# Gate spreads as one 256-column product per token, and the end of stage E

## The chip, the cores and the metric

The kernel runs on one core of a Trainium2 chip. The metric is the device time of one execution in microseconds. The five engines that matter are TensorE (PE in the profile, PEld for its weight loads), VectorE (DVE), ScalarE (ACT), GpSimd (POOL) and the transfer queues, of which most are filled by SyncE (SP).

## What is computed

One layer of a decoder over 520 tokens (512 of a prompt, 8 of a decoding batch): attention and a state-space layer, then a mixture of 16384 single-neuron experts, 128 x 128, chosen by product keys. The change touches the mixture alone:

```python
def peer(h, w_q, sub_keys, u_tab, v_tab):
    ...
        s1, i1 = lax.top_k(s[:, :, 0], PEER_TOPK)
        s2, i2 = lax.top_k(s[:, :, 1], PEER_TOPK)
        ...
        top_s, top_p = lax.top_k(cand_s, PEER_TOPK)
        idx = jnp.take_along_axis(cand_i, top_p, axis=-1)
        gate = jax.nn.softmax(top_s, axis=-1)
        u = u_tab[idx]
        act = jax.nn.gelu(jnp.einsum('thkd,td->thk', u, hb).astype(jnp.float32))
        v = v_tab[idx].astype(jnp.float32)
        return jnp.einsum('thk,thkd->td', gate * act, v).astype(h.dtype)
```

Each token has 8 heads with 16 chosen experts each, 128 (first key, second key, gate) triples.

## The kernel before, in words

The program has five stages one behind the other, with a barrier and a clearing of semaphores between any two. A, M and D are the projections, attention and state space, and the output projection. Stage E makes the query products and the first half of the mixture, stage F the second half and the last norm.

All dense products split an operand into a part in the rounded 32-bit format (float32r) and a rest in the same format, and add three products: high x high, low x high, high x low. A block of weights (1 MB, a "unit") is loaded by SP into `raw`, ScalarE writes its rounded part `wh` in two halves (`split_hi`, L122), GpSimd subtracts it in four instructions of 128 x 512 into the rest `wl` (`split_lo`, L129), TensorE multiplies. Two units are in flight: ScalarE starts on unit u + 2 when TensorE has finished unit u.

The mixture treats tokens in two ways. 360 of the 520 tokens are dense: in stage E TensorE forms their product with each of the 16384 expert rows of u (128 units, `dense`, L1560 to L1570, 48 products of 360 columns each), ScalarE applies the gelu (L1483) and stores the result to memory (L1485). For the other 160 (128 "A" tokens and 32 "x" tokens) the chosen rows are gathered one per token and step by an indirect transfer that GpSimd issues (L1423 and L1430, 128 steps each, spread over the units by `gathers_by`), into rings of four buffers (`GW`, `GX`). VectorE forms their dots (`dot`, L1729, 2048 elements against PSUM; `dot_x`, L1736, 512 elements, both inputs in SBUF). The gather of step k waits for the dot of step k - 4.

The dense tokens need their gates as a full 128 x 128 matrix per token. `spread` builds it on TensorE: for one token the stationary operand holds, for each of its 128 chosen triples, a row that is one at the second key, the moving operand a row that is the gate at the first key. `one_hots` (L1738 to L1749) makes both on VectorE by comparing a line of 0..127, kept in PSUM, with the triple's numbers. There are 90 batches of four tokens, one behind each of 90 units of stage E, in three groups of thirty (`batch_of`, units 16 to 109 with two free ones between groups). The products are 32-bit ones of 128 columns, and TensorE carries each out as two records. ScalarE copies the four results from PSUM to `gs` (L1512) with a stride, and stores `gs` after every six batches (L1516). `keyrow` has two sets of rows, so `one_hots` of batch b waits for the spread of batch b - 2. VectorE's order of a unit in the code is: dots, dots of x, compares, and in eight units a piece of the choice for the next group of tokens (`offer_choice`, L1702 to L1705).

Stage E ends with the split of the second block of stage F, the sum of x's partial dots on TensorE (L1621), two gelus on ScalarE (L1518, L1520) and two multiplications by the gates on VectorE (L1794, L1796). Stage F begins with loads on SP, the weighing of the first eight stored rows (VectorE L2004, ScalarE L1899, VectorE L1977, one behind another), then runs 128 units like E's against the rows of v, with three `raw` buffers.

Of the kernel before, what the change touches and what calls it, by code (L numbers as in the profile page):

```python
# [8 lines left out]
F32 = mybir.dt.float32  # L9
# [8 lines left out]
P = 128  # L18
# [50 lines left out]
def common(nc, ctx, ins, outs):  # L69
# [18 lines left out]
    m.gains = at("gains", [P, 3, KT]); m.eps = at("eps", [P, 1]); m.pages = at("pages", [1, P], I32); m.lam = at("lam", [P, 8])  # L88
# [1266 lines left out]
def stage_e(nc, m, ins, outs):  # L1355
# [10 lines left out]
    act0, g0, actx, gX, pf, tpa, p0 = row("act0", 0), row("g0", 1), row("actx", 2), row("g_x", 3), row("pf", 4), row("tpa", 5, U32), [row("p00", 6), row("p01", -1)]  # L1366
# [3 lines left out]
    m.idxx = at("idxx", [P, HK], I32); m.wx = at("wx", [P, HK]); m.xsel = at("xsel", [P, P + 1])  # L1370
# [16 lines left out]
    S = {n: sem("e_" + n) for n in "keys_in iota_in root_ready h_ready h_hi h_lo tok_turned tok_kept query_ready scored scores_kept head_taken chain idx_ready h_placed iota_placed best_shifted exps_ready choice_ready choice_turned keys_ready spread_done side_kept dotted dots_gelu gates_stored x_turned x_kept x_dotted x_summed xsel_in".split()}  # L1387
# [4 lines left out]
    batch_of = {E0 + SPAN * (b // per) + b % per: b for b in range(NB * BB)}  # L1392
    choice_of = {E0 - 1 + SPAN * j: j for j in range(DT)}
    piece_of = {SPAN * j - 12 + 4 * part: (j, part) for j in range(1, DT) for part in range(4)}
    with nc.Block() as block:
# [15 lines left out]
        def _(pool):  # L1411
# [22 lines left out]
        def _(act):  # L1434
# [42 lines left out]
            side = 0  # L1477
            for e in range(N_EXP):
                u, s = U_EXP_U + e, e % 2
                split_hi(m, act, u + 2, s, (u + 2) // 2, (m.mm_done, u + 3))  # L1480
# [5 lines left out]
                if e == 0:  # L1486
# [3 lines left out]
                    act.wait_ge(S["iota_in"], 16)  # L1490
                    act.activation(m.acc[:, 1, 1, 0:P], iota[:, :], ACT.Copy).then_inc(S["iota_placed"], 1)
# [6 lines left out]
                if e in choice_of:  # L1498
# [3 lines left out]
                    side += 1  # L1502
                if e in batch_of:
                    b = batch_of[e]
                    blk, n = b // BB, b % BB
                    act.wait_ge(S["spread_done"], b + 1)
                    if n == 0:
                        if blk >= 2:
                            act.wait_ge(S["gates_stored"], 16 * (blk - 1))
                        if blk == 0:  # L1510
                            act.wait_ge(S["h_placed"], 4)
# [12 lines left out]
        def _(pe):  # L1524
# [47 lines left out]
            def turn_choice(j, ready, side):  # L1572
                pe.wait_ge(S["choice_ready"], ready)
                if side is not None:
                    pe.wait_ge(S["side_kept"], side)
# [582 lines left out]
```

## Time and profile before

| | |
|---|---|
| Median of the runs shown | 3469.01 us (three: 3463.54, 3469.01, 3469.45) |
| The profiled execution, own time | 3468.28 us |
| Its span | 3466.5 us |
| TensorE busy | 3310.6 us, 96% |
| VectorE busy | 2403.1 us, 69% |
| GpSimd busy | 2286.2 us, 66% |
| ScalarE busy | 1107.3 us, 32% |
| Transfers, mean | 280 GB/s |

Stage E lies between about 1100 and 2420 us of the span, its units with spreads between 1449 and 2270 us, stage F behind 2425 us. "Busy" of TensorE is a modelled duration of overlapping products, so distances between starts are what counts. A bracket at the end of a timeline row gives the idle time before the instruction and what ended it; an x4 row is four instructions merged, with their time in all.

### The profile page before, as it was taken

The numbers are of one execution on the slowest core, as the hardware profiler recorded it, in microseconds if no ns is written. First come the engines' busy times: TensorE is split into PE (matmuls) and PEld (weight loads), VectorE is DVE, ScalarE is ACT, GpSimd is POOL, SyncE is SP. The second block draws the span as 40 slices with busy tenths as digits, with TensorE's granted clock in tenths as the row PEclk, the third lists the DMA queues.
The fourth block names the chain that finished last, engine by engine and source line by source line (L and its number), as shares of the span: only waits on it lengthen the run. The fifth ranks groups of instructions, "written<-read, shape, count | busy, mean of one in ns | idle before, by whom it ended". The sixth has DMA issues, their size and how long they took to land. (4 is left out here: it accounts for less than half of the span.)

```text
span 3466.5 us, 58063 instructions
## 1 busy us (share of the span) xinstructions
PE 3310.6 (96%) x22639; PEld 3131.8 (90%) x22639; DVE 2403.1 (69%) x4061; ACT 1107.3 (32%) x1501; POOL 2286.2 (66%) x1861
## 2 busy tenths in 40 slices
PE   7999987888998999999999999998999999999997
PEld 7988854556998999999999999998999999999997
DVE  7842323324313899998598666646799999999984
ACT  4211123234223224344444444432332232332332
POOL 2533308002443347888898888887799999999983
PEclk9999989999998999999999999999999999999998
DMA  4598977574332223788988898987998998989972
GB/s 157 191 373 312 348 293 250 212 239 164 145 118 88 85 85 135 280 327 330 345 332 341 331 346 325 347 341 279 377 381 347 382 368 359 382 355 372 375 283 98
DMA packets 239612, 970.33 MB, mean 280 GB/s; under 512 B 44913, under 2 KB 92658, under 8 KB 160626
## 3 DMA queue, kind: packets, MB, share of 16 engines
q1 hardware_dynamic: 110546, 553.25, 42.5%
q0 software_dynamic: 57344, 335.58, 24.1%
q10 hardware_dynamic: 71520, 78.87, 6.7%
q8 instruction: 119, 1.95, 0.2%
q14 instruction: 83, 0.68, 0.1%
HBM read 891.32 MB, written 73.92 MB: 278 GB/s over the span
## 5 line engine op out<-in xcount | busy, mean ns | idle before, releaser
L129 POOL TENSOR_TENSOR wl<-raw,wh 128x512 fp32r<-128x512 f32 x776 | 1049.9, 1386 | 641.7 <-ACT wh L122 640.0
L122 ACT ACTIVATE wh<-raw 128x1024 fp32r<-128x1024 f32 x396 | 397.5, 1051 | 1223.7 <-PE acc L149 581.2
L1567 PE MATMUL acc<-hh,wh 128*128 128x360 f32 x2048 | 677.5, 331 | 6.6 <-POOL wl L129 6.6
L1946 PE MATMUL acc<-vh,wh 128*128 128x360 f32 x2048 | 668.9, 327 | 12.9 <-DVE vl L1977 12.8
L1569 PE MATMUL acc<-hh,wl 128*128 128x360 f32 x2048 | 671.0, 328 | 0.0
L1948 PE MATMUL acc<-vh,wl 128*128 128x360 f32 x2048 | 670.8, 328 | 0.0
L1568 PE MATMUL acc<-hl,wh 128*128 128x360 f32 x2048 | 670.8, 328 | 0.0
L1947 PE MATMUL acc<-vl,wh 128*128 128x360 f32 x2048 | 669.2, 327 | 0.0
L1876 POOL TENSOR_TENSOR wl<-raw,wh 128x512 fp32r<-128x512 f32 x442 | 564.2, 1310 | 50.2 <-ACT wh L1914 48.2
L147 PE MATMUL acc<-hh,wh 128*128 128x256 f32 (+1 forms) x1920 | 548.5, 286 | 6.4 <-DVE tt L427 3.8
L148 PE MATMUL acc<-hl,wh 128*128 128x256 f32 (+1 forms) x1920 | 545.5, 284 | 0.0
L149 PE MATMUL acc<-hh,wl 128*128 128x256 f32 (+1 forms) x1920 | 544.1, 283 | 0.0
L1914 ACT ACTIVATE wh<-raw 128x1024 fp32r<-128x1024 f32 x252 | 253.2, 1052 | 604.7 <-PE acc L1948 546.4
L1729 DVE SCALAR_TENSOR_TENSOR ug<-ug,aux 128x2048 f32<-128x2048 f32 x128 | 291.8, 2283 | 175.2 <-DMA ug<-expert_u,idx 169.2
L1946 PEld LDWEIGHTS acc<-vh,wh 128*128 128x128 f32 x2048 | 385.5, 188 | 13.9 <-issue 12.9
L1567 PEld LDWEIGHTS acc<-hh,wh 128*128 128x128 f32 x2048 | 384.3, 188 | 9.2 <-issue 9.2
L147 PEld LDWEIGHTS acc<-hh,wh 128*128 128x128 f32 x1920 | 365.2, 190 | 22.8 <-issue 22.7
L1947 PEld LDWEIGHTS acc<-vl,wh 128*128 128x128 f32 x2048 | 385.2, 188 | 0.0
L1568 PEld LDWEIGHTS acc<-hl,wh 128*128 128x128 f32 x2048 | 385.1, 188 | 0.0
L1948 PEld LDWEIGHTS acc<-vh,wl 128*128 128x128 f32 x2048 | 385.0, 188 | 0.0
L1569 PEld LDWEIGHTS acc<-hh,wl 128*128 128x128 f32 x2048 | 384.9, 188 | 0.0
L148 PEld LDWEIGHTS acc<-hl,wh 128*128 128x128 f32 x1920 | 364.9, 190 | 0.1
(364 smaller groups left out, 5103.2 us busy)
## 6 DMA issues: line engine op xcount, KB each, us to landing
raw<-units SPq DMA_DIRECT2D x324, 1024.0 KB
kr<-cache_k SPq DMA_DIRECT2D x128, 512.0 KB, 6.6
vr<-cache_v SPq DMA_DIRECT2D x128, 512.0 KB, 5.6
expert_acts<-ast ACTq DMA_DIRECT2D x128, 180.0 KB
expert_gates<-gs ACTq DMA_DIRECT2D x15, 1536.0 KB
g<-expert_gates SPq DMA_DIRECT2D x16, 1440.0 KB, 10.7
a<-expert_acts SPq DMA_DIRECT2D x30, 720.0 KB, 13.9
output_steps<-qo ACTq DMA_DIRECT2D x16, 288.0 KB, 7.1
```

The source lines that it names most:

```text
L122: act.activation(m.wh[s][:, k:k + KT // 2, :], m.raw[s][:, k:k + KT // 2, :], ACT.Copy).then_inc(m.hi_done, 1)
L129: x = pool.tensor_tensor(m.wl[s][:, part, :], m.raw[s][:, part, :], m.wh[s][:, part, :].bitcast(F32), ALU.subtract)
L147: pe.matmul(o, m.wh[s][:, k, :], rhs_hi[:, k, c0:c0 + n], start=(k == k_range[0]), stop=False)
L148: pe.matmul(o, m.wh[s][:, k, :], rhs_lo[:, k, c0:c0 + n], start=False, stop=False)
L149: mm = pe.matmul(o, m.wl[s][:, k, :], rhs_hi[:, k, c0:c0 + n], start=False, stop=(k == k_range[-1]))
L1567: pe.matmul(o, m.wh[s][:, k, :], m.hh[:, k, N0:T], start=(k == 0), stop=False)
L1568: pe.matmul(o, m.wh[s][:, k, :], m.hl[:, k, N0:T], start=False, stop=False)
L1569: mm = pe.matmul(o, m.wl[s][:, k, :], m.hh[:, k, N0:T], start=False, stop=(k == KT - 1))
L1876: x = pool.tensor_tensor(wl[v % RW][:, part, :], raw[v % RW][:, part, :], wh[v % RW][:, part, :].bitcast(F32), ALU.subtract)
L1946: pe.matmul(tile_acc[r % AW], wh[b][:, VT * e + d, :], vh[g % 2][:, e, :], start=(e == 0), stop=False)
L1947: pe.matmul(tile_acc[r % AW], wh[b][:, VT * e + d, :], vl[g % 2][:, e, :], start=False, stop=False)
L1948: mm = pe.matmul(tile_acc[r % AW], wl[b][:, VT * e + d, :], vh[g % 2][:, e, :], start=False, stop=(e == GRP - 1))
```

## The change

The spread becomes one product per token in the rounded format with 256 moving columns: the first 128 are the key row times the gate's low part, the other 128 the key row times the gate (written rounded). The two halves of the result stand side by side in PSUM, in two banks for the four tokens of a batch. VectorE adds them while it copies them to `gs` (`keep_gates`, two reductions of 512 elements), a step that ScalarE did before. VectorE makes the key rows of four tokens with two compares of 512 elements, whose line now lies in SBUF, and ScalarE scales them by the gate's low part and by the gate (eight operations of 128 columns), waiting for the compares in the unit before. There is one set of key rows. VectorE's order of a unit becomes: keep the last batch's gates, compares, dots, dots of x, choice pieces. The store of `gs` moves one unit later.

At the seam, the split of the second block of stage F moves from E's end into F (`rest(1)` on GpSimd, its rounding on ScalarE behind the eight first roundings of the weighed rows and three loads). The sum of x's dots, the two gelus and the two multiplications move into F too: TensorE's product to its very start, the gelus behind ScalarE's rounding of unit 2, the multiplications behind VectorE's first rests. The dots are summed directly into `w0` and `wx`; the gates of the gathered tokens lie where the page table and qs were.

```diff
-    keyrow = at("keyrow", [P, KT, T], F32, off=hx + KT * T * 4)
+    keyrow = at("keyrow", [P, KT, T], F32R, off=hx + KT * T * 4)
+    glo, ghr = row("glo", 0), row("ghr", 1, F32R)
...
+    store_of = {E0 + SPAN * (blk // RUN) + BB * (blk % RUN) + BB: blk for blk in range(NB)}
-                split_lo(m, pool, u + 2, u % 2)
+                if e < N_EXP - 1:
+                    split_lo(m, pool, u + 2, u % 2)
-                split_hi(m, act, u + 2, s, (u + 2) // 2, (m.mm_done, u + 3))
+                act.wait_ge(m.mm_done, u + 3)
+                if e < N_EXP - 1:
+                    split_hi(m, act, u + 2, s, (u + 2) // 2, (m.mm_done, u + 3))
-                    act.wait_ge(S["iota_in"], 16)
-                    act.activation(m.acc[:, 1, 1, 0:P], iota[:, :], ACT.Copy).then_inc(S["iota_placed"], 1)
...
-                if e in batch_of:
-                    b = batch_of[e]
-                    blk, n = b // BB, b % BB
-                    act.wait_ge(S["spread_done"], b + 1)
...
-                    act.activation(gs[blk % 2][:, :, 4 * n:4 * n + 4].rearrange("p e t -> p t e"), m.acc[:, 0, 1, :].rearrange("p (t e) -> p t e", t=4), ACT.Copy).then_inc(S["side_kept"], 1)
-                    if n == BB - 1:
-                        act.wait_ge(S["side_kept"], side)
-                        act.dma_start(m.gD[:, :, blk, :], gs[blk % 2][:, :, :].rearrange("p (g e) n -> p g (e n)", g=NG)).then_inc(S["gates_stored"], 16)
-            act.wait_ge(S["dotted"], HK)
-            act.activation(act0[:, :], act0[:, :], ACT.Gelu_apprx_tanh).then_inc(S["dots_gelu"], 1)
-            act.wait_ge(S["x_summed"], 1)
-            act.activation(actx[:, :], m.acc[:, 0, 1, 0:HK], ACT.Gelu_apprx_tanh).then_inc(S["dots_gelu"], 1)
+                if e in store_of:
+                    blk = store_of[e]
+                    act.wait_ge(S["gates_kept"], 2 * BB * (blk + 1) + 1)
+                    act.dma_start(m.gD[:, :, blk, :], gs[blk % 2][:, :, :].rearrange("p (g e) n -> p g (e n)", g=NG)).then_inc(S["gates_stored"], 16)
+                if e + 1 in batch_of:
+                    b = batch_of[e + 1]
+                    if b % per == 0:
+                        act.wait_ge(S["gates_split"], b // per + 1)
+                    act.wait_ge(S["keys_made"], b + 1)
+                    for t in range(4):
+                        act.activation(keyrow[:, 8 + t, 0:P], keyrow[:, t, 0:P].bitcast(F32), ACT.Copy, scale=glo[:, 4 * b % DW + t:4 * b % DW + t + 1])
+                    for t in range(4):
+                        x = act.activation(keyrow[:, 12 + t, 0:P], keyrow[:, t, 0:P].bitcast(F32), ACT.Copy, scale=gt[:, 0, 4 * b + t:4 * b + t + 1])
+                    x.then_inc(S["keys_ready"], 1)
...
-            def spread(n, b, side):
+            def spread(b, j):
                 pe.wait_ge(S["keys_ready"], b + 1)
-                pe.wait_ge(S["side_kept"], side)
-                for t in range(4):
-                    r = 4 * (n % 2) + t
-                    mm = pe.matmul(m.acc[:, 0, 1, P * t:P * t + P], keyrow[:, r, 0:P], keyrow[:, 8 + r, 0:P], start=True, stop=True)
+                pe.wait_ge(S["side_kept"], j + 1)
+                for h in range(2):
+                    if h == 0:
+                        pe.wait_ge(S["gates_kept"], b * 2 + 1)
+                    for t in range(2 * h, 2 * h + 2):
+                        mm = pe.matmul(m.acc[:, h, 1, 2 * P * (t % 2):2 * P * (t % 2) + 2 * P].rearrange("p (x n) -> p x n", x=2), keyrow[:, 4 + t, 0:P], keyrow[:, 8 + t:13 + t:4, 0:P], start=True, stop=True)
                 mm.then_inc(S["spread_done"], 1)
...
-            pe.wait_ge(S["side_kept"], (per + 1) * DT)
-            pe.wait_ge(S["x_dotted"], HK)
-            pe.matmul(m.acc[:, 0, 1, 0:HK], m.xsel[:, 0:P], actx[:, :], start=True, stop=True).then_inc(S["x_summed"], 1)
+            pe.wait_ge(S["gates_kept"], 2 * per * DT + 1)
...
+                                         accum_out=m.w0[:, k:k + 1]).then_inc(S["dotted"], 1)
...
+                dve.scalar_tensor_tensor(ugx[k % GX][:, :], ugx[k % GX][:, :], 1.0, hq[:, :], ALU.mult, ALU.mult, accum_out=m.wx[:, k:k + 1]).then_inc(S["x_dotted"], 1)
+
+            def split_gates(j):
+                dve.wait_ge(S["side_kept"], j + 1)
+                ch(dve.tensor_copy(ghr[:, 0:DW], gt[:, 0, DW * j:DW * j + DW]))
+                dve.tensor_tensor(glo[:, 0:DW], gt[:, 0, DW * j:DW * j + DW], ghr[:, 0:DW].bitcast(F32), ALU.subtract).then_inc(S["gates_split"], 1)
+
+            def keep_gates(b):
+                blk, n = b // BB, b % BB
+                dve.wait_ge(S["spread_done"], b + 1)
+                if n == 0 and blk >= 2:
+                    dve.wait_ge(S["gates_stored"], 16 * (blk - 1))
+                for h in range(2):
+                    parts = m.acc[:, h, 1, :].rearrange("p (t x e) -> p t e x", t=2, x=2)
+                    dve.tensor_reduce(gs[blk % 2][:, :, 4 * n + 2 * h:4 * n + 2 * h + 2].rearrange("p e t -> p t e"), parts, AX.X, ALU.add).then_inc(S["gates_kept"], 1)
-                n = b % BB
-                if b == 0:
-                    dve.wait_ge(S["iota_placed"], 1)
-                if b >= 2:
-                    dve.wait_ge(S["spread_done"], b - 1)
-                line = m.acc[:, 1, 1, 0:P]
-                for t in range(4):
-                    c, r = 4 * b + t, 4 * (n % 2) + t
-                    dve.tensor_scalar(keyrow[:, r, 0:P], line, gt[:, 2, c:c + 1], None, ALU.is_equal)
-                    x = dve.tensor_scalar(keyrow[:, 8 + r, 0:P], line, gt[:, 1, c:c + 1], gt[:, 0, c:c + 1], ALU.is_equal, ALU.mult)
-                x.then_inc(S["keys_ready"], 1)
+                line = iota[:, :].unsqueeze(1).broadcast_to([P, 4, P])
+                for x in range(2):
+                    i = dve.tensor_tensor(keyrow[:, 4 * x:4 * x + 4, 0:P], line, gt[:, 1 + x, 4 * b:4 * b + 4].unsqueeze(2).broadcast_to([P, 4, P]), ALU.is_equal)
+                i.then_inc(S["keys_made"], 1)
...
             for e in range(N_EXP):
+                if e - 1 in batch_of:
+                    keep_gates(batch_of[e - 1])
+                if e in batch_of:
+                    b = batch_of[e]
+                    if b % per == 0:
+                        split_gates(b // per)
+                    one_hots(b)
                 while k < dots_by(e):
                     dot(k)
                     k += 1
                 while kx < dots_x_by(e):
                     dot_x(kx)
                     kx += 1
-                if e in batch_of:
-                    b = batch_of[e]
-                    if b % per == 0:
-                        dve.wait_ge(S["side_kept"], (per + 1) * (b // per) + 1)
-                    one_hots(b)
                 if e in piece_of:
                     offer_choice(*piece_of[e])
...
-            dve.wait_ge(S["dots_gelu"], 1)
-            ch(dve.tensor_tensor(m.w0[:, :], act0[:, :], g0[:, :], ALU.mult))
-            dve.wait_ge(S["dots_gelu"], 2)
-            ch(dve.tensor_tensor(m.wx[:, :], actx[:, :], gX[:, :], ALU.mult))
+            dve.wait_ge(S["dotted"], HK)
+            dve.wait_ge(S["x_dotted"], HK)
...
+            def rest(v):
+                for k in range(0, KT * 3 // 4 if rest_shared(v) else KT, KT // 4):
+                    if k % (KT // 2) == 0:
+                        pool.wait_ge(m.hi_done, (U_EXP_V + v) * 2 + (1 + 2 * k // KT))
+                    part = slice(k, k + KT // 4)
+                    x = pool.tensor_tensor(wl[v % RW][:, part, :], raw[v % RW][:, part, :], wh[v % RW][:, part, :].bitcast(F32), ALU.subtract)
+                x.then_inc(m.lo_done, 1)
+
+            rest(1)
+                    rest(j + 2)
...
+            act.wait_ge(raw_in[1], raw_count(1))
+            for k in range(0, KT, KT // 2):
+                act.activation(wh[1][:, k:k + KT // 2, :], raw[1][:, k:k + KT // 2, :], ACT.Copy).then_inc(m.hi_done, 1)
...
+            def rounded(v):
+
+            rounded(2)
+            act.activation(m.w0[:, :], m.w0[:, :], ACT.Gelu_apprx_tanh).then_inc(S["w_gelu"], 1)
+            act.wait_ge(S["x_summed"], 1)
+            act.activation(m.wx[:, :], m.acc[:, 1, 0, 0:HK], ACT.Gelu_apprx_tanh).then_inc(S["w_gelu"], 1)
+            for v in range(2, N_EXP):
+                if v > 2:
+                    rounded(v)
...
+            pe.matmul(m.acc[:, 1, 0, 0:HK], m.xsel[:, 0:P], m.wx[:, :], start=True, stop=True).then_inc(S["x_summed"], 1)
...
+            dve.wait_ge(S["w_gelu"], 2)
+            dve.tensor_tensor(m.w0[:, :], m.w0[:, :], m.g0[:, :], ALU.mult).then_inc(S["w_ready"], 1)
+            dve.tensor_tensor(m.wx[:, :], m.wx[:, :], m.gX[:, :], ALU.mult).then_inc(S["w_ready"], 1)
+            dve.wait_ge(S["w_ready"], 2)
```

## Rows read from the trace of the kernel before

**Rows 1.** The page: the span.

```profile
span 3466.5 us, 58063 instructions
```

**Rows 2.** Busy us by engine (PE, PEld, DVE, ACT, POOL), granted clock, transfers.

```profile
1449.30:1697.67 248.37, 247.61 (x1568) 247.31 (x1569) 218.99 (x388) 104.58 (x110) 214.34 (x176) 1.00 0.88 333
```

**Rows 3.** TensorE's waits, whole span: us in total, times, longest.

```profile
PE acc L1946 <- DVE vl L1977: 12.8, 1, 12.8
...
PE acc L1567 <- POOL wl L129: 6.6, 9, 1.8
```

**Rows 4.** Timeline of TensorE: two spreads (start, us, line, operation, tiles).

```profile
1600.54 1.05 PE L1585 MATMUL acc<-keyrow 128*128 128x128 f32 x8
...
1609.37 0.38 PE L1585 MATMUL acc<-keyrow 128*128 128x128 f32 x2
```

**Rows 5.** Timeline of ScalarE: gelus of the last units of E.

```profile
2407.72 0.45 ACT L1483 ACTIVATE ast<-acc 128x360 f32<-128x360 f32 x1
...
2415.66 0.45 ACT L1483 ACTIVATE ast<-acc 128x360 f32<-128x360 f32 x1
```

**Rows 6.** Timeline of TensorE: products of 256 columns, first and 36th.

```profile
1179.78 0.28 PE L148 MATMUL acc<-hl,wh 128*128 128x256 f32 x1
...
1183.93 0.28 PE L147 MATMUL acc<-hh,wh 128*128 128x256 f32 x1
```

**Rows 7.** Timeline of GpSimd around the same two spreads.

```profile
1601.32 0.95 POOL L1430 DMA_INDIRECT ugx<-expert_u,idxx  x1 [0.31 <-issue]
1602.28 5.04 POOL L129 TENSOR_TENSOR wl<-raw,wh 128x512 fp32r<-128x512 f32 x4
...
1609.01 0.95 POOL L1430 DMA_INDIRECT ugx<-expert_u,idxx  x1 [0.30 <-issue]
1610.77 2.54 POOL L129 TENSOR_TENSOR wl<-raw,wh 128x512 fp32r<-128x512 f32 x2 [0.81 <-ACT wh L122]
```

**Rows 8.** Timeline of VectorE in the same unit.

```profile
1603.38 4.50 DVE L1736 SCALAR_TENSOR_TENSOR ugx<-ugx,hq 128x512 f32<-128x512 f32 x1
...
1607.82 0.68 DVE L1736 SCALAR_TENSOR_TENSOR ugx<-ugx,hq 128x512 f32<-128x512 f32 x1
```

**Rows 9.** Timeline of GpSimd in a unit that began with idling.

```profile
1847.71 5.95 POOL L129 TENSOR_TENSOR wl<-raw,wh 128x512 fp32r<-128x512 f32 x4 [0.90 <-ACT wh L122]
...
1855.07 0.95 POOL L1430 DMA_INDIRECT ugx<-expert_u,idxx  x1 [0.31 <-issue]
```

**Rows 10.** Timeline of VectorE in that unit.

```profile
1849.23 1.58 DVE L1736 SCALAR_TENSOR_TENSOR ugx<-ugx,hq 128x512 f32<-128x512 f32 x1
```

**Rows 11.** Timelines: a compare with both inputs in SBUF, and a GpSimd train.

```profile
1510.38 1.21 DVE L1702 TENSOR_TENSOR eq<-pf,iota 120x1024 f32<-120x1024 f32 x1
...
1550.60 2.22 DVE L1702 TENSOR_TENSOR eq<-pf,iota 120x1024 f32<-120x1024 f32 x1
...
1547.93 6.03 POOL L129 TENSOR_TENSOR wl<-raw,wh 128x512 fp32r<-128x512 f32 x4 [0.62 <-ACT wh L122]
```

**Rows 12.** Line L1705 by itself: ns min/median/max, first and last start.

```profile
L1705 DVE TENSOR_REDUCE gx<-eq x12: 1219/1220/1221, 1410.0 to 1864.1; 120x64 f32<-120x1024 f32 x12
```

**Rows 13.** Timeline of ScalarE: two short operations at E's end.

```profile
2416.51 0.31 ACT L1518 ACTIVATE act<-act 128x128 f32<-128x128 f32 x1 [0.40 <-ACT ast L1483]
2416.73 0.26 ACT L1520 ACTIVATE actx<-acc 128x128 f32<-128x128 f32 x1
```

**Rows 14.** Timelines of GpSimd, VectorE, TensorE and ScalarE at the seam.

```profile
2414.88 5.03 POOL L129 TENSOR_TENSOR wl<-raw,wh 128x512 fp32r<-128x512 f32 x4 [2.89 <-ACT wh L122]
2434.57 2.55 POOL L1876 TENSOR_TENSOR wl<-raw,wh 128x512 fp32r<-128x512 f32 x2 [14.65 <-ACT wh L1914]
...
2424.88 0.98 DVE L2004 TENSOR_TENSOR a<-a,g 128x360 f32<-128x360 f32 x2 [6.08 <-PEq L2075]
...
2426.66 0.64 PE L1946 MATMUL acc<-vh,wh 128*128 128x360 f32 x1 [12.79 <-DVE vl L1977]
...
2437.36 2.01 ACT L1914 ACTIVATE wh<-raw 128x1024 fp32r<-128x1024 f32 x2 [1.91 <-PE acc L1948]
```

More of the change, by code:

```diff
@@ L1570, in dense, with turn_choice @@
                 mm.then_inc(m.mm_done, 1)
[L1572 removed]
+            def turn_choice(j, ready, kept):
                 pe.wait_ge(S["choice_ready"], ready)
[L1574 to L1575 removed]
+                if kept is not None:
+                    pe.wait_ge(S["gates_kept"], kept)
                 for x in range(3):
@@ L1609, in _ @@
                         dense(i * BB + (E0 + SPAN * j + n), n % 2)
-                        spread(n, i * BB + (per * j + n), i * BB + (per * j + n + 1 + j))
+                        spread(i * BB + (per * j + n), j)
                 if j + 1 < DT:
@@ L1613, in _ @@
                         dense(E0 + SPAN * j + per + s, s)
-                    turn_choice(j + 1, j + 2, (per + 1) * (j + 1))
+                    turn_choice(j + 1, j + 2, 2 * per * (j + 1) + 1)
             rest = E0 + SPAN * (DT - 1) + per
@@ L1827, in stage_f @@
     yx = m.acc[:, 1, 0, :]
-    S = {n: sem("g_" + n) for n in "raw2_in rest_done weighed weighed_hi weighed_lo sum_added tile_done rows_added y_kept y_turned squares_ready squares_added squares_summed root_ready out_ready out_stored x_added x_turned".split()}
+    S = {n: sem("g_" + n) for n in "x_summed w_gelu w_ready raw2_in rest_done weighed weighed_hi weighed_lo sum_added tile_done rows_added y_kept y_turned squares_ready squares_added squares_summed root_ready out_ready out_stored x_added x_turned".split()}
     raw_in = m.raw_in + [S["raw2_in"]]
@@ L1868, in _ @@
         def _(pool):
+            def rest(v):
[6 more added lines that the diff above has]
+            rest(1)
             for j in range(N_EXP):
                 if j < N_EXP - 2:
-                    v = j + 2
-                    for k in range(0, KT * 3 // 4 if rest_shared(v) else KT, KT // 4):
-                        if k % (KT // 2) == 0:
-                            pool.wait_ge(m.hi_done, (U_EXP_V + v) * 2 + (1 + 2 * k // KT))
-                        part = slice(k, k + KT // 4)
-                        x = pool.tensor_tensor(wl[v % RW][:, part, :], raw[v % RW][:, part, :], wh[v % RW][:, part, :].bitcast(F32), ALU.subtract)
-                    x.then_inc(m.lo_done, 1)
+                    rest(j + 2)
                 for k in range(rows_by(j), rows_by(j + 1)):
@@ L1907, in square @@
                 act.activation(sq[:, k % 4, :], m.xt[:, k, :], ACT.Square).then_inc(S["squares_ready"], 1)
-            for v in range(2, N_EXP):
+            def rounded(v):
                 act.wait_ge(raw_in[v % RW], raw_count(v))
```

28 lines of the change are left out of this document (11 added, 17 removed).

## The prediction

> **What bounds the kernel now.** I read first the page (busy times, and which lines hold them), then the busy times of the stretch that the change touches, then the waits of TensorE, and last the timelines of all engines over a few units of that stretch. The span is 3466.5 us [rows 1]. Over 28 of the ninety units of stage E that carry a spread it is busy 247.61 of 248.37 us at a granted clock of 1.00, while VectorE works 219.0 us and GpSimd 214.3 us of them [rows 2]. In stage E it waits 6.6 us for GpSimd's low halves, and at the seam to stage F once 12.8 us [rows 3]. So TensorE sets the pace, but two other engines have only a tenth of it to spare, and the change moves work among exactly these.
>
> One unit with a spread takes 1609.37 - 1600.54 = 8.83 us from spread to spread [rows 4]. A unit without one takes 2415.66 - 2407.72 = 7.94 us, by the distance of two gelus of the late units [rows 5]. The spread thus costs 0.89 us of the path, in 8 records.
>
> **The change part by part.** I count from S, the start of a unit's spread on TensorE.
>
> *TensorE.* Four products with 256 moving columns replace eight records of 128. With 256 columns in this format 35 products start within 1183.93 - 1179.78 = 4.15 us, 0.119 us each [rows 6]. Four cost 0.48 us; I leave the 0.07 us that the old spread cost beyond its eight records of 0.10 us. The spread becomes 0.55 us and the unit 8.50 us, if nothing is late: 90 x 0.33 = 30 us less. Bounds for one product: 0.10 us (the old records) and 0.165 us (360 columns), so the unit lies between 8.4 and 8.7 us.
>
> *GpSimd.* Its first instruction on the low half starts when ScalarE has rounded half a block, 1610.77 - 1609.37 = 1.40 us after S [rows 4, 7]. The four of them, a train, take 5.04 us without a break, then come the gathers: 1607.32 to 1609.96 us is 2.6 us for one of each kind, so a plain unit is 7.7 us of work. Every eighth unit gathers one expert row more, every seventh one x row more, each 0.31 + 0.95 = 1.26 us [rows 7]: 0.34 us in the mean, 8.0 us in all. The change leaves this work alone, but not what it meets.
>
> *VectorE.* Removed are eight small compares (scalar and line in PSUM). Added are two reductions of 512 elements from PSUM and two compares of 512 elements whose two inputs both lie in SBUF. A reduction of 1024 takes 1.22 us [rows 12]; half of that and a little start is 0.65 us, the two 1.3 us. The PSUM read and a written stride of 96 bytes are shown by no row for this engine; the bounds are 0.3 us each (the slope hidden behind the neighbour) and 1.2 us each (the full 1024). I take 0.65 us, as the same operation is the nearest row. An operation on 512 elements with two inputs takes 0.68 us alone [rows 8].
>
> These compares don't run alone. The operation on x rows (both inputs in SBUF, 512 elements) took 4.50 us when it began inside a train of GpSimd, and ended 0.56 us after the train [rows 7, 8]. Other trains let it in: there it took 1.58 us, beginning its work when the current instruction of GpSimd ended, and the train, with a second such meeting, grew to 5.95 us [rows 9, 10]. A compare with broadcast inputs in SBUF, the form that the change adds, behaves alike: 1.21 us alone, 2.22 us in a train that grew to 6.03 us [rows 11]. I went through all such meetings in stage E, some sixty. What parts them is how the train began: when it started right behind a gather (GpSimd late, no idle before it, 35 of 114 trains, [rows 7] at 1602.28), VectorE stood until the train was over; when GpSimd had idled for ScalarE first ([rows 9], 0.90 us), VectorE came in between.
>
> The new order puts the compares in that place every time. The reductions wait for the spread (done about S + 0.8: last product 0.36, its 0.28 us and the signal), and end at S + 2.1. The train runs from S + 1.4 at the earliest. Before, the compares read a line in PSUM and could be made up to two units ahead, since they waited only for the spread before last.
>
> *ScalarE* then scales eight rows of 128 columns: 0.22 us apart, 0.31 us long for such an operation [rows 13]. These have a scale per partition; bounds 1.8 us and 3.2 us (0.31 with a tenth more each), taken 2.5, with signals 2.6 us. The old 1.45 us copy of the spread goes. ScalarE issues nothing else meanwhile; behind its new wait stands the next unit's rounding, and so the next train.
>
> *A fresh unit* (GpSimd had idled): the compares come in behind the first and second instruction and end at S + 4.9, keys at S + 7.5, before the product's turn at 8.50. The train and its gathers last 1847.71 to 1856.02 = 8.31 us [rows 9], till S + 9.71, which is 1.21 us into the next unit: just before 1.40, so that one is fresh too. It takes 8.50 us. But one more gather (27 units in 100) puts the end at 2.5 us, and the next train follows without idling.
>
> *A lost unit*: train from 1.5 to 2.5 us after S. From 1.5 it ends at 6.5, the compares at 6.5 + 0.56 + 0.68 = 7.7, the keys at 10.3. From 2.3 the first compare slips in at 2.1, the train runs 2.7 to 7.7, the second ends at 8.3, the keys at 10.9. The spread waits for them: 10.3 to 10.9 us. And it is passed on. The ring of expert rows has four places: a gather waits for the dot four before it. By the schedule of the code, four units of eight need for that the first dot of the same unit, which on VectorE now stands behind the compares: 8.3 + 2.28 = 10.6, gathers till 10.7 + 2.5 = 13.2, that is 2.3 us into the next unit: lost again. Before, VectorE ran ahead and waited for landings instead.
>
> Counting eight units: the one with two gathers makes the next lost, its blocked neighbours keep that for three more and into a fifth; the extra x row falls on one more or two. 5.5 of 8 lost: (5.5 x 10.9 + 2.5 x 8.5) / 8 = 10.15 us. Ninety units: 90 x (10.15 - 8.83) = +119 us. With 3 of 8 it is 9.4 us, +51; with 8 of 8, 10.9 us, +186. Choice pieces (eight, on VectorE after the dots) and the split of the gate (three) are inside these ends.
>
> *Seam.* Stage E ends with GpSimd at 2414.88 + 5.03 = 2419.9; VectorE's first work of F is at 2424.88 [rows 14]. The last block's split moves into F, so E ends with ScalarE's gelu and issue, about 2414.6: 5.3 us sooner. But the moved split now stands behind eight roundings and three transfers' issue on ScalarE. Before, GpSimd began F at 2434.57, with ScalarE's first rounding there [rows 14]; the moved one takes that place, 2429.3, and ends at 2434.3. TensorE, at 2421.4 instead of 2426.66, is done with its first unit at 2432.0 (before 2437.3 [rows 14]): it waits 2.4 us. Net -3 us. Past it on SP comes the load of the block that goes into the freed buffer, issued 2.5 us later than before; bounds -5.3 and 0. The gelus, the small x product and the two weight multiplies move behind the first units, beside TensorE's 10 us; without that cover they are about 1 us.
>
> **Sum.** 3466.5 + 119 - 3 = 3582.5 us of span, 1.8 us around it as in the profiled execution (3468.28), and the median of the runs lies 0.7 us above that: 3585 us.
>
> **Rivals.** (1) *VectorE is always let in at the next instruction.* The Trainium skill, "SBUF — State Buffer", section "SBUF: two separate sides", says of the pair of ports that VectorE and GpSimd share that whichever instruction starts first has it for the whole instruction; taken literally, nobody waits longer than one instruction. [rows 7, 8] speak against it, [rows 9, 10] for it. As a mechanism of this kernel: every unit is fresh, GpSimd's unit is 8.31 + 0.34 = 8.65 us, below the 8.83 us of before. Then 90 x 0.18 to 90 x 0.33 = 16 to 30 us less, with the seam 3436 to 3450 us, about 3443. It decides by the share of lost units: 8.50 + 2.4 x share passes 8.83 at 0.14; above one lost unit in seven the kernel is slower. (2) *Few lost*: trains start a little later than I reckon, so that only the extra gathers lose, or reductions of 1.2 us delay the keys a little past 8.5: 8.8 to 9.2 us, 3463 to 3500 us. Here belongs also that the product isn't cheaper. (3) *TensorE's clock.* It now idles about 2 us in most units. In this stretch it was granted 1.00 [rows 2]; at the start of F, behind 12.8 us of idling [rows 3], products ran slower. Should it fall to 1.2 GHz within these units, dense work of 7.9 us grows and the time passes 3650 us.
>
> **How the numbers follow.** Lost race, as forecast: 0.68. Rival 1: 0.14. Rival 2: 0.13, half of it within the bound of 0.2% (7 us, about what a measurement of this kernel can tell). Rival 3 and worse: 0.05. Faster 0.16, same 0.08, slower 0.76. The range 3450 to 3645 takes the forecast's own 3517 to 3645, all of rival 2, and leaves out most of rival 1 and rival 3.
>
> **What would show it.** In the profile after: spreads of four records in 0.5 us; compares whose mean is far above 0.7 us, many ending 0.5 us after a train; TensorE waiting for the key rows (written by ScalarE) in more than half of the units, 100 us or more in all; VectorE's waits for landings of expert rows gone and GpSimd waiting for dots instead; the seam's wait 7 to 8 us with a second one of 2 us behind it. I am wrong if the compares come in at the next instruction whatever the train, or if GpSimd never starts one without idling.

## The result

The changed kernel takes 3632.99 us (median, 3629.0 to 3638.2) against 3466.28 us for the kernel before on the same chip: ratio 1.0481, 95% interval [1.0464, 1.0498]. It is 4.8% slower. The forecast was 3585 us with a range of 3450 to 3645 us, and slower as the likeliest side. Direction and mechanism held; the forecast was 48 us short of the measured time, and that is what there is to explain beside the mechanism itself.

The page of the changed kernel, span [rows 1]:

```profile
span 3627.2 us, 57751 instructions
```

The busy times of the first third of stage E's units with a spread (columns as in [rows 2]):

```profile
1439.54:1758.57 319.03, 262.81 (x1510) 256.90 (x1509) 299.26 (x267) 137.69 (x320) 224.28 (x183) 0.94 0.74 272
```

Before, TensorE was busy 99.7% of such a stretch. Now it is busy 82%, the transfers fell from 0.88 to 0.74, and it is VectorE that is busy 94%. That looks like a VectorE bound, but much of this time is no work, as the lines of its two new operations show (count, then min/median/max in ns):

```profile
L1755 DVE TENSOR_TENSOR keyrow<-iota,gt x180: 662/1055/5908, 1430.8 to 2430.4; 128x512 fp32r<-128x512 f32 x180
L1750 DVE TENSOR_REDUCE gs<-acc x180: 785/812/833, 1440.2 to 2435.0; 128x256 f32<-128x512 f32 x180
```

A compare takes 0.66 us alone and up to 5.91 us; the mean is 2.28 us (404.1 us for 180). The reduction, which reads PSUM, never leaves 0.79 to 0.83 us. The waits say what becomes late by it, TensorE's first (in all, times, longest; nothing of this kind stands in [rows 3]), then ScalarE's, then GpSimd's:

```profile
PE acc L1587 <- ACT keyrow L1519: 159.7, 62, 9.6
PE acc L1567 <- POOL wl L130: 8.4, 9, 3.3
```

```profile
ACT keyrow L1517 <- DVE keyrow L1755: 445.4, 81, 13.6
```

```profile
POOL ug L1429 <- DVE ug L1729: 133.5, 42, 4.6
POOL ugx L1436 <- DVE ugx L1736: 60.2, 20, 9.0
```

The chain is there in order: TensorE waits for the key rows that ScalarE scales, ScalarE for VectorE's compares, and GpSimd for the dots queued behind the compares. In the kernel before GpSimd waited 5.2 and 0.6 us for the two kinds of dots. VectorE waited 169.2 us for landings of expert rows there, 128.2 us of it among the units with spreads; among them that wait is gone, and 28.0 us are left behind them.

**Where the 160.7 us of span went.** 87 distances from spread to spread lie within the three groups of tokens. 16 are 8.4 us, two more under 9.9, 17 are 9.9 to 10.6 (eight 10.4), 40 are 10.6 to 11.3 (most 11.1), nine 11.3 to 14 (most 12.7), and three over 14 (18.0 to 18.3). Their mean is 10.78 us against 8.83: 87 x 1.95 = 169 us. The two distances over a group's end grew from 25.0 to 28.3 us, 7 us together. The seam gave 6 us back, stage F took 2 us more, and everything ahead of the first spread ran 10 us quicker in this execution. The sum is 162. Of the 10 us, 3.3 arose at the first query products of stage E, where the granted clock of 8 us was 0.58 before (1120 to 1128 us) and 1.00 now (1114 to 1122 us). Whether the change has a part in that no run shows.

**One lost unit.** GpSimd, VectorE and ScalarE between the spreads of 1605.32 and 1615.75, then the spreads:

```profile
1606.93 5.04 POOL L130 TENSOR_TENSOR wl<-raw,wh 128x512 fp32r<-128x512 f32 x4
```

```profile
1605.99 1.44 DVE L1750 TENSOR_REDUCE gs<-acc 128x256 f32<-128x512 f32 x2 [1.15 <-PE acc L1587]
1607.21 5.92 DVE L1755 TENSOR_TENSOR keyrow<-iota,gt 128x512 fp32r<-128x512 f32 x2
1613.05 2.28 DVE L1729 SCALAR_TENSOR_TENSOR ug<-ug,aux 128x2048 f32<-128x2048 f32 x1
```

```profile
1613.17 1.28 ACT L1517 ACTIVATE keyrow<-keyrow,glo 128x128 fp32r<-128x128 f32 x4 [5.21 <-issue]
1614.35 1.26 ACT L1519 ACTIVATE keyrow<-keyrow,gt 128x128 fp32r<-128x128 f32 x4
```

```profile
1605.32 0.64 PE L1587 MATMUL acc<-keyrow 128*128 128x256 f32 x4
1615.75 0.74 PE L1587 MATMUL acc<-keyrow 128*128 128x256 f32 x4 [1.87 <-ACT keyrow L1519]
```

The train has no bracket: GpSimd did not idle before it, and it starts 1.61 us after the spread and 0.28 us before the compares. The two compares together last 5.92 us and end 1.16 us after the train (1613.13 against 1611.97): the first ends half a microsecond after the train, the second runs alone. ScalarE's eight operations take 2.44 us, and TensorE has waited 1.87 us.

The most frequent length is 11.1 us. VectorE and GpSimd in such a unit, after the spread of 1712.58:

```profile
1714.58 6.47 DVE L1755 TENSOR_TENSOR keyrow<-iota,gt 128x512 fp32r<-128x512 f32 x2
```

```profile
1714.87 5.02 POOL L130 TENSOR_TENSOR wl<-raw,wh 128x512 fp32r<-128x512 f32 x4
```

Here the first compare began 0.29 us before the train's first instruction, during the gather ahead of it, and was caught all the same: it ended at 1720.45, 0.56 us after the train. Over all units with spreads 68 compares and x dots were lengthened by a train that began without idling. 67 of them ended 0.55 or 0.56 us after the train, and 39 had begun up to 0.37 us before it. Of 37 that were lengthened by a train before which GpSimd had idled, 32 ended inside it.

**One fresh unit**, after the spread of 1439.54, GpSimd and VectorE:

```profile
1440.96 5.96 POOL L130 TENSOR_TENSOR wl<-raw,wh 128x512 fp32r<-128x512 f32 x4 [0.39 <-ACT wh L123]
```

```profile
1441.45 3.06 DVE L1755 TENSOR_TENSOR keyrow<-iota,gt 128x512 fp32r<-128x512 f32 x2
```

Here GpSimd had idled for ScalarE. The compares need 3.06 us, not 5.92, and it is the train that grows, to 5.96 us. The next spread comes after 8.41 us without a wait.

**A unit made long by the clock.** Not every long distance is a wait for keys. The columns of three units as in [rows 2] (a late one, then two in time), and ScalarE's last scaling in the second:

```profile
1605.32:1615.75 10.43, 8.56 (x54) 8.27 (x53) 9.76 (x7) 4.95 (x12) 8.51 (x8) 1.00 0.88 326
1672.86:1682.89 10.03, 10.03 (x52) 10.03 (x53) 7.64 (x10) 4.57 (x11) 7.95 (x6) 0.83 0.42 151
1682.89:1691.30 8.41, 8.41 (x54) 8.41 (x53) 7.25 (x8) 4.82 (x11) 6.84 (x5) 1.00 0.56 232
```

```profile
1679.76 1.27 ACT L1519 ACTIVATE keyrow<-keyrow,gt 128x128 fp32r<-128x128 f32 x4
```

In the second unit the keys are there at 1681.03, 8.16 us after the spread, and TensorE never waits. It is busy for 10.03 us because its granted clock is 0.83 in the mean: part of the unit ran at 1.2 instead of 2.4 GHz. Five of the 87 distances are of this kind (keys 5.8 to 8.2 us after the spread, 10.0 to 10.8 us long). So of the 69 that are over 9.9 us, the keys were late in 64: in 60 TensorE waits for them, and in four (keys at 10.1 to 10.3 us) its slowed work hides the wait.

### The profile page after: what moved, and what is told of

It is laid out like the page before. It is cut to its first block and busy times, and to the rows that moved or that the text cites. A ratio compares the mean times of both kernels' runs of the same rounds, so it can differ in the third digit from the quotient of the medians.

```text
span 3627.2 us, 57751 instructions
## 1 busy us (share of the span) xinstructions
PE 3315.8 (91%) x22279; PEld 3122.4 (86%) x22279; DVE 2638.5 (73%) x3707; ACT 1189.8 (33%) x2130; POOL 2286.4 (63%) x1861
## 3 DMA queue, kind: packets, MB, share of 16 engines
q8 instruction: 119, 1.95, 0.2%
## 5 line engine op out<-in xcount | busy, mean ns | idle before, releaser
L1567 PE MATMUL acc<-hh,wh 128*128 128x360 f32 x2048 | 687.0, 335 | 8.4 <-POOL wl L130 8.4
L1568 PE MATMUL acc<-hl,wh 128*128 128x360 f32 x2048 | 685.4, 335 | 0.0
L1569 PE MATMUL acc<-hh,wl 128*128 128x360 f32 x2048 | 684.4, 334 | 0.0
L1567 PEld LDWEIGHTS acc<-hh,wh 128*128 128x128 f32 x2048 | 397.4, 194 | 11.7 <-issue 11.2
L1755 DVE TENSOR_TENSOR keyrow<-iota,gt 128x512 fp32r<-128x512 f32 x180 | 404.1, 2284 | 0.0
L1568 PEld LDWEIGHTS acc<-hl,wh 128*128 128x128 f32 x2048 | 397.7, 194 | 0.0
L1569 PEld LDWEIGHTS acc<-hh,wl 128*128 128x128 f32 x2048 | 397.3, 194 | 0.0
L148 PEld LDWEIGHTS acc<-hh,wh 128*128 128x128 f32 x1920 | 364.0, 190 | 22.6 <-issue 21.7
L149 PEld LDWEIGHTS acc<-hl,wh 128*128 128x128 f32 x1920 | 363.8, 189 | 0.1
## 6 DMA issues: line engine op xcount, KB each, us to landing
g<-expert_gates SPq DMA_DIRECT2D x16, 1440.0 KB, 11.6
```

The costliest lines, as they stand in the source:

```text
L148: pe.matmul(o, m.wh[s][:, k, :], rhs_hi[:, k, c0:c0 + n], start=(k == k_range[0]), stop=False)
L149: pe.matmul(o, m.wh[s][:, k, :], rhs_lo[:, k, c0:c0 + n], start=False, stop=False)
L1567: pe.matmul(o, m.wh[s][:, k, :], m.hh[:, k, N0:T], start=(k == 0), stop=False)
L1568: pe.matmul(o, m.wh[s][:, k, :], m.hl[:, k, N0:T], start=False, stop=False)
L1569: mm = pe.matmul(o, m.wl[s][:, k, :], m.hh[:, k, N0:T], start=False, stop=(k == KT - 1))
L1755: i = dve.tensor_tensor(keyrow[:, 4 * x:4 * x + 4, 0:P], line, gt[:, 1 + x, 4 * b:4 * b + 4].unsqueeze(2).broadcast_to([P, 4, P]), ALU.is_ ...
```

## The experiments

All times are medians of runs beside the kernel before on the same chip.

### Is it the port, or VectorE's load? The line read from PSUM

```diff
-                line = iota[:, :].unsqueeze(1).broadcast_to([P, 4, P])
+                line = m.aux[:, 0, 0:P].unsqueeze(1).broadcast_to([P, 4, P])
```

Order, waits and sizes stay (one wait for that tensor comes in ahead of the first batch); only one of the compares' two inputs leaves SBUF.

> The changed kernel, but the two compares of a unit read their line from PSUM, where another tensor lies (128 columns of the tokens' rows), so the gates come out wrong; every instruction, its size and every wait stay. Theory (the compares lose time because both inputs lie in SBUF, against GpSimd's train): compares fall from 2.28 us mean to about 0.7 us, nearly all units with a spread take 8.4 to 8.6 us instead of 10.8, TensorE's wait for key rows falls from 160 us to under 15, and the time is 3425 to 3450 us. Rival (the chain spread, reductions, compares, scaling is too long whatever port it uses, since each batch now waits for the spread before it): compares shorten, but TensorE still waits in most units, the time stays above 3580 us.

Measured: 3446.58 us, ratio 0.9946 [0.9928, 0.9964]. 79 of the 87 distances are 8.4 us, the mean of all is 8.64. TensorE's wait is 17.7 us where under 15 was expected; the rest came as the theory said. The compares and TensorE's waits for the keys:

```profile
L1757 DVE TENSOR_TENSOR keyrow<-aux,gt x180: 670/681/735, 1434.4 to 2243.9; 128x512 fp32r<-128x512 f32 x180
```

```profile
PE acc L1587 <- ACT keyrow L1519: 17.7, 6, 5.2
```

Not one of 180 compares is above 0.74 us, though 41 of the 94 trains among these units began without idling. The 186 us between this kernel and the changed one are the price of two SBUF inputs beside GpSimd, with all that follows from it. VectorE has the same operations to do and is not too slow for them. The x dots, which keep two SBUF inputs, still stand for microseconds (2.99 us at 1603.18), and it costs nothing.

### Is it that the train has no break? The train in steps

```diff
+        if steps is not None and k < KT - KT // 4:
+            steps[1] += 1
+            x.then_inc(steps[0], 1)
+            pool.wait_ge(steps[0], steps[1])
```

Each instruction of GpSimd's train now waits for a semaphore that the one before it raises. The compares are those of the changed kernel.

> The changed kernel, but in stage E each GpSimd instruction of a train waits for a semaphore of the one before it, so that a late train has gaps too. Theory (a late train keeps the port only because its instructions stand ready one behind another): VectorE comes in after the current instruction in every unit; no compare takes over 2 us; trains grow to 6.2 to 6.6 us, GpSimd becomes the bound at 8.9 to 9.2 us a unit, the time falls by 120 to 170 us, to 3460 to 3510 us. Rival (VectorE waits until the train ends whatever its gaps): time within 20 us of 3633 us or above, compares still near 2.3 us mean.

Measured: 3500.27 us, ratio 1.0101 [1.0081, 1.0121]; mean distance 9.12 us, 39 of them 8.4 us and 33 between 8.6 and 9.9. GpSimd and VectorE in a unit where GpSimd was late, as in the lost unit above:

```profile
1510.14 6.08 POOL L130 TENSOR_TENSOR wl<-raw,wh 128x512 fp32r<-128x512 f32 x4
```

```profile
1510.31 3.38 DVE L1760 TENSOR_TENSOR keyrow<-iota,gt 128x512 fp32r<-128x512 f32 x2
```

```profile
L1760 DVE TENSOR_TENSOR keyrow<-iota,gt x180: 670/781/2423, 1437.8 to 2289.8; 128x512 fp32r<-128x512 f32 x180
```

The train began 0.17 us before the compares and without idling, and still the two ended 3.38 us later, in the middle of it. The longest compare falls from 5.91 to 2.42 us (18 of 180 are over 2 us, where none was expected), the mean from 2.28 to 1.25 us, and TensorE's wait for keys from 159.7 to 33.7 us. So what shuts VectorE out for a whole train is that the four instructions follow each other without a wait. The steps aren't free: three trains that neither a compare nor an x dot met last 5.38 us, against 5.04 us, and TensorE's waits for low halves rise to 23.1 us. Both effects together stay 1% above the kernel before, so the steps are a test and no remedy.

### Is the lateness passed on through the dots? Dots before compares

```diff
+                while k < dots_by(e):
+                    dot(k)
+                    k += 1
+                while kx < dots_x_by(e):
+                    dot_x(kx)
+                    kx += 1
                 if e - 1 in batch_of:
                     keep_gates(batch_of[e - 1])
```

(and the two loops taken out behind the compares.)

> The changed kernel, but VectorE's order of a unit is dots, dots of x, reductions, compares. Theory (a lost unit is passed on because the gathers wait for a dot that stands behind the compares): GpSimd's waits for dots fall from 194 us in all to under 60 us, the share of lost units falls from 7 of 8 to about half, mean unit 9.5 to 10.2 us, time 3530 to 3590 us. Rival (the passing on has nothing to do with the ring; every unit loses by itself): mean unit stays at 10.8 us, time 3620 to 3650 us.

Measured: 3532.65 us, ratio 1.0194 [1.0176, 1.0213]: 100 us of the 167 us come back. Mean distance 9.65 us, 33 of 8.4 us instead of 16, 13 near 11.1 instead of 40. GpSimd waits for dots 4.9 us in all, where it was 133.5 + 60.2 us, and only 33 of the 94 trains start without idling, where it was 69 of 94. All this is as the theory had it. Compares still meet trains (median 1.72 us, TensorE waits 84.3 us for keys in 42 spreads), so this takes the passing on away and leaves the meeting. Keys are late in 39 of the 87 units now. In 13 more they came 6.9 to 8.2 us after the spread and the unit was still some 10 us long (9.8 to 10.7), at a granted clock below 1.00: 22 us of the 67 that remain.

### The seam alone

The kernel before, with the changed kernel's seam to stage F and nothing else of the change.

> The kernel before with the seam's part of the change alone (last split, sum of x's dots, gelus and multiplications moved into stage F). By the step of the prediction: 5.3 us sooner at the start of F, 2.4 us lost again at its second unit, 3 us faster in all (0 to 5.3), ratio 0.9991 (0.9985 to 1.000). The profile of the changed kernel says the first product of F comes 6.2 us sooner and the second unit waits 1.6 us: 4 to 5 us. Rival (nothing gained, the transfers at the start of F bound it): 0 us.

Measured: 3462.64 us, ratio 0.9986 [0.9977, 0.9995], or 4.9 us less (1.7 to 8.0), as the profile of the changed kernel had said (4 to 5) and rather more than the forecast's 3. TensorE and VectorE at the seam of the changed kernel:

```profile
2583.45 0.46 PE L1958 MATMUL acc<-wx,xsel 128*128 128x128 f32 x2 [3.16 <-PEq L2103]
...
2585.39 0.64 PE L1970 MATMUL acc<-vh,wh 128*128 128x360 f32 x1 [1.49 <-DVE vl L2001]
...
2597.82 0.43 PE L1970 MATMUL acc<-vh,wh 128*128 128x360 f32 x1 [1.62 <-POOL wl L1883]
```

The one wait of 12.79 us [rows 14] has become 3.16 + 1.49 us, and the second unit waits 1.62 us more for GpSimd's low half.

### The compares made ahead

The first test shows what the product is worth if its keys are in time. This version gets that without PSUM: the compares of the next unit's keys stand behind the dots of the present unit, and the second half of the keys has two sets of rows.

```diff
+                    if b > 0:
+                        act.wait_ge(S["spread_done"], b)
...
-                    one_hots(b)
...
+                if e + 1 in batch_of and batch_of[e + 1] % per != 0:
+                    one_hots(batch_of[e + 1])
```

> The changed kernel, but the compares for the next unit's keys are made behind the dots of the present unit, with a second set of rows for the second half of the keys, so that they no longer stand between a spread and the same unit's late GpSimd work. The compares still have both inputs in SBUF, and GpSimd's trains are as they were. My theory (what costs time in the changed kernel is that a compare which meets an unbroken train ends after it, and that the keys' turn comes only one unit later) expects that the compares now mostly fall behind the train, or, where they meet one, still end before ScalarE is wanted: 75 or more of the 87 distances from spread to spread at about 8.4 us as in the run with the line in PSUM, TensorE's wait for keys under 30 us in all, and a time of 3425 to 3455 us, that is 10 to 40 us faster than the kernel before. A rival: VectorE is simply full (dots, compares, reductions and the blocked time come to more than 8.4 us a unit), and then the wait only changes its place: the mean distance stays at 9 us or more and the time at 3490 us or above.

Measured: 3442.76 us, ratio 0.9941 [0.9927, 0.9954], so 20.6 us faster than the kernel before and, by the two ratios, 187 us faster than the change as made. 78 of the 87 distances are 8.4 us, mean 8.60. VectorE in one unit (spread at 1599.77), the compares that write `keyrow` (the other 45 write the second set, `key2b`), and TensorE's waits:

```profile
1604.50 4.32 DVE L1740 SCALAR_TENSOR_TENSOR ugx<-ugx,hq 128x512 f32<-128x512 f32 x1
1608.76 0.07 DVE L1740 DVE_READ_ACCUMULATOR ugx<-ugx,hq 128x1 f32 x1
1608.76 0.68 DVE L1762 TENSOR_TENSOR keyrow<-iota,gt 128x512 fp32r<-128x512 f32 x1
1609.36 0.68 DVE L1762 TENSOR_TENSOR key2b<-iota,gt 128x512 fp32r<-128x512 f32 x1
```

```profile
L1762 DVE TENSOR_TENSOR keyrow<-iota,gt x135: 675/680/5885, 1434.7 to 2236.6; 128x512 fp32r<-128x512 f32 x135
```

```profile
PE acc L1591 <- ACT keyrow L1522: 7.9, 3, 2.8
PE acc L1591 <- DVE gs L1754: 7.8, 3, 4.0
```

The train now catches the x dot (4.32 us), for which nobody waits, and the compares run behind it in 0.68 us each (one of the 180 is still caught, 5.89 us). The gain adds up: 87 x (8.83 - 8.60) = 20 us, 5 us from the seam, less 5 us at the two group ends (27.5 us each, before 25.0). VectorE's load was not the limit here either.

### What the choice pieces cost

The changed kernel, with the pieces of the second and third group left out:

```diff
-                if part == 0:
-                    weigh(2 + j, gx[0:DW, 3 * j, 0:P])
-                find_keys(2 + j, lambda c: gx[0:DW, 3 * j + 1 + c, 0:P], part)
+                if j == 0:
+                    if part == 0:
+                        weigh(2 + j, gx[0:DW, 3 * j, 0:P])
+                    find_keys(2 + j, lambda c: gx[0:DW, 3 * j + 1 + c, 0:P], part)
```

> The changed kernel without the choice pieces of the second and third group of tokens that VectorE does between the units of stage E (weighing the answer and finding the experts' keys): these groups use the first group's choice, so the gates of their tokens are not the reference's, while all loads, products, compares and spreads are kept. In the changed kernel twelve of the 87 distances from spread to spread are over 11.3 us, and I hold that they are the units with pieces. Theory: without pieces no distance is over 11.3 us, the others stay as they are (about 8.4, 10.4 and 11.1 us, mean 10.3), and the time falls by 30 to 45 us to about 3590 to 3600 us. Rival: the long distances come from something else (a group's start, loads of the next block), or a piece is only added to units that are late anyway: then the time falls by under 10 us and distances of 12 us or more remain.

Measured: 3605.09 us, ratio 1.0406 [1.0390, 1.0422], 0.0075 below the changed kernel's, which is 26 us (the two intervals allow 18 to 34). The expectation is half right. The distances of 18 us are gone, so these were pieces. But eleven of 11.6 to 12.8 us remain, each right behind a unit with two expert dots: they have another cause. VectorE and GpSimd in one of them (spreads at 1641.03 and 1653.77):

```profile
1638.34 2.27 DVE L1730 SCALAR_TENSOR_TENSOR ug<-ug,aux 128x2048 f32<-128x2048 f32 x1
1640.55 0.08 DVE L1730 DVE_READ_ACCUMULATOR ug<-ug,aux 128x1 f32 x1
1640.55 2.28 DVE L1730 SCALAR_TENSOR_TENSOR ug<-ug,aux 128x2048 f32<-128x2048 f32 x1
1642.76 0.08 DVE L1730 DVE_READ_ACCUMULATOR ug<-ug,aux 128x1 f32 x1
1642.76 5.93 DVE L1737 SCALAR_TENSOR_TENSOR ugx<-ugx,hq 128x512 f32<-128x512 f32 x1
1648.62 1.43 DVE L1751 TENSOR_REDUCE gs<-acc 128x256 f32<-128x512 f32 x2
```

```profile
1643.12 5.01 POOL L130 TENSOR_TENSOR wl<-raw,wh 128x512 fp32r<-128x512 f32 x4
```

It is the unit with two expert dots. The compares ended late in one train, the two dots take 4.5 us, and the x dot behind them is caught by the next unit's train, although it began 0.36 us before it. It stands 5.93 us, and with it the reductions and compares of that unit, which should have begun at 1642. One unit is blocked twice. With the dots ahead of the compares only three of the 87 distances are above 11.3 us, which fits, as the x dot then comes before the train.

## Why the prediction held, and where it fell short

**The mechanism: right.** The compares stand while a train runs that began without idling. Taking an input out of SBUF removes it, and so does breaking the train. The rival by which VectorE is let in at the next instruction (3443 us) fell. The Trainium skill, "SBUF — State Buffer", section "SBUF: two separate sides", says that a VectorE operation with two SBUF inputs and a GpSimd operation that reads SBUF exclude each other, and that the one which starts first has the shared ports for its whole instruction. That the two collide the runs bear out: a compare took up to 5.91 us with two SBUF inputs and at most 0.74 us with one. That the first to start has the ports they don't: 39 operations that began before the train stood until it was over. Nor was one instruction the most that was waited for, as the prediction's first rival read it: it was four, unless the four were parted by waits.

**A lost unit: right within 0.2 us, in part by luck.** Train from 1.5 us after the spread: it was 1.61 us, compares to 7.81 (forecast 7.7), product 10.43 (10.3). Train from 2.3 us: the forecast let the first compare in ahead of the train, which would then run from 2.7 to 7.7, and made the second wait. Eight units went that way (train from 2.7 to 2.9 us, products at 10.9 to 11.1, forecast 10.9). In 25 the first compare was caught though it had begun ahead of the train, and the second ran alone behind it. In the unit of 1712.58 the train ran from 2.29 to 7.31 us after the spread, the compares ended at 8.47 (forecast 8.3), and the product came at 11.08. That this other way ends within 0.2 us of the forecast's is luck.

**A fresh unit: the spread was sized a little high.** Keys at 7.46 us after the spread (7.5), train of 5.96 us (5.95). The unit is 8.41 us where 8.50 was forecast: the spread costs 8.41 - 7.94 = 0.47 us, not 0.55. The 0.07 us added for the old spread's surplus wasn't there.

**The share of lost units: a little low.** 5.5 of 8 were forecast, 60 of 87. The keys were late in 64, 5.9 of 8. The four more are 4 x 2.4 = 10 us. Why there are four more isn't shown. The x dots, with two SBUF inputs too, don't meet trains more often than before: 14 of 107 among these units took over 1 us, where it was 42 of 109. The rival with few lost units fell with this count.

**The clock: assumed full, and it wasn't.** Between the first spread and the last, 994 us, the granted clock was at 1.2 GHz in 22 stretches, 99 us together; in the 819 us of the kernel before, never. Each stretch began within one of TensorE's waits of 2.3 to 9.6 us or up to 1.6 us behind its end. 18 other waits of such lengths had none. In the units of 11.1 us it cost nothing, as TensorE then waited 0.9 instead of 2.4 us. In the five units with keys in time it cost 8 us against the forecast. This is the prediction's third rival, in part: the clock did fall within the units, for a tenth of the time, and not to the price of over 3650 us that the rival put on it.

**The unit with two dots: a case that was missing.** Twelve distances are over 11.3 us, together 38 us above the forecast's 10.9 each. Eleven of them follow a unit with two expert dots. Seven of these hold no choice piece and are 12.45 to 12.75 us long, 1.8 us above 10.9. At that price the two dots account for 20 of the 38 us.

**The choice pieces: the step that failed most.** They were put "inside these ends" without a price of their own. That had been true of a kernel in which VectorE ran ahead. Behind the change nothing is ahead: a piece that stands before the reductions delays the keys by its whole length. The other 18 of the 38 us are in the five units of the twelve that hold a piece; the three of 18 us are among them. Leaving the pieces out took 26 us away (18 to 34).

**Reductions: 0.81 us each, not 0.65**, well inside the bounds of 0.3 and 1.2; a lost unit hardly notices, since the compares wait for the train anyway. **ScalarE's keys:** 0.39 us for one, 0.30 us apart, 2.44 us for the eight, against 2.5.

**Group ends:** 3.3 us each longer, where the sum counted them as plain units with 1.3 us. At a group's start the gate's split, the compares and the scaling come before the first spread one after the other, with nothing made ahead.

**The seam: -3 forecast, -4.9 measured** (-1.7 to -8.0), within its bounds. The second unit's wait was 1.6 us, not 2.4, and the first 3.16 + 1.49 us, not 7 to 8.

Over the profiled execution: 10 us for four more late units, 8 for the clock and 38 for the twelve long ones, less 2 for all others, is 54 us. With 3 us at the group ends, 3 us less at the seam, 2 us in F and 10 us less ahead of the spreads it is 46 us more than the forecast's 3582.5, against 44.7 measured. The measured 3633 us lie 12 us below the end of the range. That end was set too low by the prediction's own sum: with 8 of 8 units lost it gives 3652 us, not 3645.

**Left open.** Why GpSimd's idling before a train lets VectorE in between its instructions later on, up to the fourth, wasn't settled. The stepped train shows that a wait between them does it, not what in the engine decides. Every train without idling also stood right behind a gather, and no run parts the two. What brings the clock down in one unit and not in the next of the same length is open too.

## What to carry to other kernels

Before moving an operation of VectorE, look up where its inputs lie and what GpSimd does at that time: with both in SBUF it may cost a whole run of GpSimd instructions and not its own 0.7 us. The cure here was order and a second buffer, so that what somebody waits for comes after the collision and what nobody waits for takes it. And when a change removes the slack of an engine, everything that the slack had hidden (pieces of other work, double steps every eighth unit) needs a price of its own.

## What was not expected of the hardware

An operation whose two inputs lie in SBUF took 5.9 us instead of 0.68 us beside four back-to-back GpSimd instructions of 1.26 us each, and 2.42 us at most when these were parted by semaphore waits. To begin first didn't help: with a train that began without idling close behind it, an operation that had begun up to 0.37 us ahead ended 0.56 us after the train. Operations with one input in PSUM were not touched (0.67 to 0.74 us), nor were reductions from PSUM (0.79 to 0.83 us). A cast with a single input in SBUF was touched, which no step of the forecast reckoned with. The same cast of a choice piece, once begun during a gather just ahead of a train (which ended at 1577.01), once during a gather that no train followed:

```profile
1571.35 5.75 DVE L1700 CAST pf<-tpa 120x128 f32<-120x128 uint32 x1
...
1839.31 0.23 DVE L1700 CAST pf<-tpa 120x128 f32<-120x128 uint32 x1
```

That adds to the price of the pieces. TensorE's clock fell to 1.2 GHz again and again in a stretch in which it waited for keys in 60 of 87 units, most often 2.4 us (22 times, 99 of 994 us), and a unit whose keys were in time then took 10.0 us or more instead of 8.41. With waits in a few units only, in the version with the compares ahead, the granted clock was 0.98 to 1.00.
